# Half-height, 512-column weight loads and four-result projection blocks in a float32 decoder trunk with an interleaved expert layer

## The reference, cut to what matters

```python
def _layer(x, conv_buf, mem_k, mem_v, p):
    mo, new_buf, vn = _mixer(_rmsnorm(x, p['g_mix']), conv_buf, p)
    x = x + mo
    x = x + _cross_attn(_rmsnorm(x, p['g_xattn']), mem_k, mem_v, p['w_xq'], p['w_xo'])
    x = x + _peer(_rmsnorm(x, p['g_ffn']), p['w_pq'], p['sub_keys'], p['peer_u'], p['peer_v'])
    return x, new_buf, vn

def _mixer(h, conv_buf, p):
    proj = jnp.einsum('bld,dn->bln', h, p['w_in'])          # 1024 -> 7 * 1024
    b_g, c_g, h_a, u, v, g_a, g_b = jnp.split(proj, SPLITS, axis=-1)
    z = c_g * h_a                                           # short convolution over tokens, 3 taps
    ...
    o_a = jnp.einsum('blc,cd->bld', b_g * conv, p['w_a_out'])
    u = jax.nn.gelu(u)
    vn = _layernorm(jax.nn.gelu(v), p['sg_ln_g'], p['sg_ln_b'])
    s = _spatial_gate(vn, p['sg_w'], p['sg_b'])
    o_b = jnp.einsum('blc,cd->bld', u * s, p['w_b_out'])
    m = jax.nn.sigmoid(g_a) * o_a + jax.nn.sigmoid(g_b) * o_b
    return jnp.einsum('bld,de->ble', m, p['w_mix_o']), new_buf, vn
```

## Time and profile before

| | |
|---|---|
| median of 3 runs | 4949.3 us (4941.9 to 4970.75) |
| span of the profiled execution | 4944.5 us |
| PE busy | 3105.5 us (63%) |
| PEld busy | 2272.9 us (46%) |
| DVE busy | 3498.1 us (71%) |
| ACT busy | 452.5 us (9%) |
| POOL busy | 2890.5 us (58%) |
| moved by DMA | 1526.96 MB, mean 309 GB/s |

### The profile page before, as it was taken

How to read it: one execution, slowest core, us unless ns; L and a number is a source line. 1 busy time by engine, 2 the same in 40 slices (tenths; PEclk the granted TensorE clock), 3 DMA queues, 4 the chain that set the end, 5 groups by cost and what they waited for, 6 DMA issues and landing times. The chain is left out here.

```text
span 4944.5 us, 35593 instructions
## 1 busy us (share of the span) xinstructions
PE 3105.5 (63%) x11812; PEld 2272.9 (46%) x11812; DVE 3498.1 (71%) x6425; ACT 452.5 (9%) x956; POOL 2890.5 (58%) x2317
## 2 busy tenths in 40 slices
PE   8998469797878666667565458977897663000000
PEld 7887336575865224556455226655785221000000
DVE  2101678676657897875678897867647888888887
ACT  1001000021101001012010001011111000000000
POOL 0000156565646675765667765656546677877786
PEclk9999789898579887888777778988778886555555
DMA  5444479899979887999999987989979888999998
GB/s 190 142 152 136 135 274 334 319 382 349 329 269 377 312 301 260 394 374 362 337 352 369 366 298 251 381 323 395 351 248 330 304 320 296 344 343 353 356 347 298
DMA packets 604880, 1526.96 MB, mean 309 GB/s; under 512 B 43412, under 2 KB 293460, under 8 KB 604696
## 3 DMA queue, kind: packets, MB, share of 16 engines
q0 software_dynamic: 331776, 1208.11, 66.2%
q1 hardware_dynamic: 272920, 316.58, 18.9%
HBM read 1517.29 MB, written 7.23 MB: 308 GB/s over the span
## 5 line engine op out<-in xcount | busy, mean ns | idle before, releaser
L573 POOL DMA_INDIRECT urow<-in_peer_u_dram,idx x1152 | 1471.3, 1277 | 1469.0 <-DVE idx L1135 622.8
L573 POOL DMA_INDIRECT vrow<-in_peer_v_dram,idx x1152 | 1417.3, 1230 | 557.8 <-issue 343.2
L1025 DVE CUSTOM_DVE_ANT_0 urow<-urow,T 128x1024 f32<-128x1024 f32 x1152 | 1370.2, 1222 | 206.0 <-DMA urow<-in_peer_u_dram,idx 155.4
L612 PE MATMUL ps<-RH,W 128*128 128x256 f32 (+1 forms) x4608 | 1192.4, 420 | 268.4 <-DVE RB L1268 85.4
L1046 DVE SCALAR_TENSOR_TENSOR acc<-vrow,wts,acc 128x1024 f32<-128x1024 f32 x858 | 1101.9, 1284 | 136.1 <-DMA vrow<-in_peer_v_dram,idx 70.9
L612 PEld LDWEIGHTS ps<-RH,W 128*128 128x128 f32 x4608 | 904.4, 197 | 535.9 <-issue 109.2
L802 PE MATMUL ps<-vrow,RV 128*128 128x512 f32 x1152 | 628.3, 706 | 441.1 <-DVE RV L1036 402.2
L802 PEld LDWEIGHTS ps<-vrow,RV 128*128 128x128 f32 x1152 | 254.8, 228 | 812.3 <-issue 534.7
L826 ACT ACTIVATE gel<-dots 128x4 f32<-128x4 f32 x288 | 58.9, 204 | 2639.7 <-DVE dots L1025 2529.2
L625 PE MATMUL ps<-W,RB 128*128 128x256 f32 (+1 forms) x1152 | 264.0, 393 | 40.9 <-DVE RB L1298 23.9
L612 PE MATMUL ps<-RB,W 128*128 128x256 f32 (+1 forms) x1024 | 266.0, 414 | 17.0 <-DMA W<-in_w_b_out_dram 16.0
(11 more groups left out here) (175 smaller groups left out, 2234.3 us busy)
## 6 DMA issues: line engine op xcount, KB each, us to landing
W<-in_w_in_dram SPq DMA_DIRECT2D x112, 1024.0 KB
W<-in_w_pq_dram SPq DMA_DIRECT2D x32, 1024.0 KB
urow<-in_peer_u_dram,idx POOLq DMA_INDIRECT x1152
vrow<-in_peer_v_dram,idx POOLq DMA_INDIRECT x1152
W<-in_w_a_out_dram SPq DMA_DIRECT2D x16, 1024.0 KB
W<-in_w_b_out_dram SPq DMA_DIRECT2D x16, 1024.0 KB
W<-in_w_mix_o_dram SPq DMA_DIRECT2D x16, 1024.0 KB
W<-in_w_xq_dram SPq DMA_DIRECT2D x16, 1024.0 KB
```

Of the source, the lines that this page charges most:

```text
L573: pool.indirect_dma_start(ring[:, j, :], None, table, bass.IndirectOffsetOnAxis(ap=idx[:, q % TSLOT, e:e + 1], axis=0)).then_inc(landed[j] ...
L612: m = pe.matmul(pf(name), slot(u)[:, k, (c % 2) * P:(c % 2) * P + P], src[:, k, 0:ncols(name[0] % 2)], start=(k == 0), stop=(k == KC - 1))
L1025: dve.tensor_tensor_reduce(urow[r, j, :], urow[r, j, :], T[r, kept, :], 1.0, 0.0, ALU.mult, ALU.add, dots[r, j:j + 1]).then_inc(u_read, 1)
```

## The change

Each load holds 512 columns and half of the contraction's rows: `UW = 512`, `KH = 4` row blocks. It is still 1 MiB, each row in HBM is 2 KiB. `project` forms a block of four results (`BLK = 4`) of one kind: it waits for four banks, then runs the first unit (row blocks 0 to 3) for all four results and then the second (row blocks 4 to 7), so that the four results are finished one after another in the second half. In the plan the first job of a block costs 5/2 of a result's cost, each other one 1/2. The kinds alternate by blocks: c, h, b, u for results 0 to 3, and then for 4 to 7, and ga, oa, gb, ob in the same way. `project_tokens` uses 512 moving columns.

The buffers follow: c goes to F1 in place of two buffers `cs`, the convolution is worked in F1, ga goes to mT, gb to four buffers `cs`, the query results `qp` lie in RV with four buffers in place of two; ACT no longer waits for DVE between c and h, nor between ga and oa. The number of ACT and DVE instructions is not changed.

```diff
-UW = 256
+UW = 512
+KH = KC // 2
+BLK = 4
 SLOTS = 6
-UF = KC * UW
+UF = KH * UW
...
-    for c in range(KC):
-        jobs += [(("c", c), "act", 1, fm), (("h", c), "dve", 1, fm), (("b", c), "dve", 1, fm), (("u", c), "act", 1, fm)]
+    def block(kind, a, owner):
+        return [((kind, BLK * a + i), owner, 1, fm / 2 if i else 5 * fm / 2) for i in range(BLK)]
+
+    for a in range(2):
+        jobs += block("c", a, "act") + block("h", a, "dve") + block("b", a, "dve") + block("u", a, "act")
...
-    for h in range(PH):
-        if h + 1 < PH:
-            jobs += [(("pq", 2 * h + 2), "act", 1, fm), (("pq", 2 * h + 3), "act", 1, fm)]
-        jobs += [(("sc", h), "act", 2, 2)]
+    jobs += block("pq", 0, "act")
+    for a in range(PH // 2):
+        if 2 * a + 2 < PH:
+            jobs += block("pq", a + 1, "act")
+        jobs += [(("sc", 2 * a), "act", 2, 2), (("sc", 2 * a + 1), "act", 2, 2)]
...
+    def add_block(p, kind, a):
+        add(p, kind, 2 * a, kind, BLK * a)
+        add(p, kind, 2 * a + 1, kind, BLK * a + BLK - 1)
...
-                    c0 = part * DM + n * UW
-                    src = A[name][layer_of(p), :, c0:c0 + UW].rearrange("(k p) n -> p k n", p=P)
+                    c0, r0 = part * DM + n // 2 * UW, n % 2 * KH * P
+                    src = A[name][layer_of(p), r0:r0 + KH * P, c0:c0 + UW].rearrange("(k p) n -> p k n", p=P)
...
+            def project(p, kind, a, src):
+
+                block = [(p, kind, BLK * a + i) for i in range(BLK)]
+                for name in block:
+                    begin(name)
+                for r in range(2):
+                    u = (p, kind, 2 * a + r)
                     await_unit(u)
-                for k in range(KC):
-                    m = pe.matmul(pf(name), slot(u)[:, k, (c % 2) * P:(c % 2) * P + P], src[:, k, 0:ncols(name[0] % 2)],
-                                  start=(k == 0), stop=(k == KC - 1))
-                end(m)
+                    for i, name in enumerate(block):
+                        for k in range(KH):
+                            m = pe.matmul(pf(name), slot(u)[:, k, i * P:(i + 1) * P],
+                                          src[:, KH * r + k, 0:ncols(p % 2)],
+                                          start=(r == 0 and k == 0), stop=(r == 1 and k == KH - 1))
+                        if r:
+                            end(m)
...
-                        for k in range(KC):
-                            m = pe.matmul(ps[0:rows, BANK[name] + a, b * UW:(b + 1) * UW],
-                                          src[:, k, i * P:i * P + rows], slot(u)[:, k, :],
-                                          start=(k == 0), stop=(k == KC - 1))
+                        for k in range(KH):
+                            m = pe.matmul(ps[0:rows, BANK[name] + a, :],
+                                          src[:, KH * r + k, i * P:i * P + rows], slot(u)[:, k, :],
+                                          start=(r == 0 and k == 0), stop=(r == 1 and k == KH - 1))
...
-                for c in range(KC):
-                    if c >= 2:
-                        emptied((p, "h", c - 2))
-                    evac((p, "c", c), cs[c % 2][:, 0:n], pf((p, "c", c)))
-                    evac((p, "u", c), F2[:, c, 0:n], pf((p, "u", c)), ACT.Gelu_apprx_tanh)
+                for a in range(2):
+                    for c in range(BLK * a, BLK * a + BLK):
+                        evac((p, "c", c), F1[:, c, 0:n], pf((p, "c", c)))
+                    for c in range(BLK * a, BLK * a + BLK):
+                        evac((p, "u", c), F2[:, c, 0:n], pf((p, "u", c)), ACT.Gelu_apprx_tanh)
```

More of the change, by code:

```diff
@@ L96, in phase_jobs @@
     jobs += [(("n", 1, i), "dve", 2, 2 if i else 14) for i in range(nt)]
-    jobs += [(("q", c), "act", 1, fm) for c in range(KC)]
+    jobs += block("q", 0, "act") + block("q", 1, "act")
     jobs += [(("s", 0), "act", 2, 4), (("s", 1), "act", 2, 4), (("pt", 0), "act", 2, 6)]
@@ L172, in plan_units @@
             add(p, "v", n, "v", nt - 1)
-        for n in range(4):
+        for a in range(2):
             for kind in "chbu":
-                add(p, kind, n, kind, 2 * n + 1)
-        for n in range(4):
+                add_block(p, kind, a)
+        for a in range(2):
             for kind in ("ga", "oa", "gb", "ob"):
-                add(p, kind, n, kind, 2 * n + 1)
+                add_block(p, kind, a)
         for n in range(4):
@@ L184, in plan_units @@
                     add(p, kind, n, kind, MC - 1)
-        for n in range(4):
-            add(p, "q", n, "q", 2 * n + 1)
+        for a in range(2):
+            add_block(p, "q", a)
         if g:
@@ L193, in plan_units @@
             add(p, "xo", n, "xo", nt - 1)
-        for h in range(PH):
-            add(p, "pq", h, "pq", 2 * h + 1)
+        for a in range(PH // 2):
+            add_block(p, "pq", a)
     return units, last
@@ L305, in decoder_step @@
         tmp = TMP[:, 340:340 + NM]
[L306 removed]
+        cs = [TMP[:, i:i + NM] for i in (0, 660, 980, 1300)]
         sgw = TMP[:, 0:DM].rearrange("p (g s) -> p g s", g=KC)
@@ L654, in trunk @@
                     project_tokens((p, "v", i), hT, i, rows)
-                for c in range(KC):
+                for a in range(2):
                     for kind in "chbu":
-                        project((p, kind, c), c, hT)
+                        project(p, kind, a, hT)
                 if g:
@@ L671, in trunk @@
                 await_evac(pe, (p, "mx", KC - 1))
[L672 to L676, removed]
+                for a in range(2):
+                    project(p, "ga", a, hT)
+                    project(p, "oa", a, F1)
+                    project(p, "gb", a, hT)
+                    project(p, "ob", a, F2)
                 await_evac(pe, (p, "ob", KC - 1))
@@ L694, in trunk @@
                 norm_transposes(1)
-                for c in range(KC):
-                    project((p, "q", c), c, hT)
+                for a in range(2):
+                    project(p, "q", a, hT)
                 await_evac(pe, (p, "q", KC - 1))
@@ L777, in trunk @@
                 norm_transposes(2)
-                for c in range(2):
-                    project((p, "pq", c), c, hT)
+                project(p, "pq", 0, hT)
                 for h in range(PH):
-                    if h + 1 < PH:
-                        for c in (2 * h + 2, 2 * h + 3):
-                            project((p, "pq", c), c, hT)
+                    if h % 2 == 0 and h + 2 < PH:
+                        project(p, "pq", h // 2 + 1, hT)
                     begin((p, "sc", h))
@@ L896, in trunk @@
                     act.wait_ge(zlo_out, 32 * (l + 1))
[L897 to L902, removed]
+                    act.wait_ge(vn_out, 16 * (l + 1))
+                emptied((p, "b", KC - 1))
+                for a in range(2):
+                    for c in range(BLK * a, BLK * a + BLK):
+                        evac((p, "ga", c), mT[:, c, 0:n], pf((p, "ga", c)), ACT.Sigmoid)
+                    for c in range(BLK * a, BLK * a + BLK):
+                        if a:
+                            emptied((p, "ob", c - BLK))
+                        evac((p, "gb", c), cs[c % BLK][:, 0:n], pf((p, "gb", c)), ACT.Sigmoid)
                 if not g:
@@ L957, in trunk @@
                 for h in range(PH):
-                    for c in range(0 if h == 0 else 2 * h + 2, min(2 * h + 4, 2 * PH)):
-                        evac((p, "pq", c), qp[c // 2 % 2][:, c % 2, 0:n], pf((p, "pq", c)))
+                    if h % 2 == 0:
+                        for c in range(0 if h == 0 else 2 * h + 4, min(2 * h + 8, 2 * PH)):
+                            evac((p, "pq", c), qp[c // 2 % 4][:, c % 2, 0:n], pf((p, "pq", c)))
                     name = (p, "sc", h)
@@ L1216, in trunk, with short_conv @@
                 ts = tmp[:, GC:NM].rearrange("p (b n) -> p b n", b=NSEQ)
-                for c in range(KC):
+                def short_conv(c):
                     def tap(j):
@@ L1251, in trunk @@
                         dve.wait_ge(zl_done, KC * l + c + 1)
-                    take((p, "b", c))
-                    done(dve.tensor_tensor(F1[:, c, 0:n], pf((p, "b", c)), tmp[:, 0:n], ALU.mult))
-                    emptied((p, "b", c))
+                for a in range(2):
+                    for c in range(BLK * a, BLK * a + BLK):
+                        short_conv(c)
+                    for c in range(BLK * a, BLK * a + BLK):
+                        take((p, "b", c))
+                        done(dve.tensor_tensor(F1[:, c, 0:n], pf((p, "b", c)), F1[:, c, 0:n], ALU.mult))
+                emptied((p, "b", KC - 1))
                 dve.wait_ge(sgb_in, 16 * (p + 1))
```

62 lines of the change are left out of this document (29 added, 33 removed).

## The result

The changed kernel takes 4992.6 us as a median (4975.7 to 5011.3, 6 runs) against 4952.9 (4937.6 to 4970.8, 6 runs) for the kernel before on the same chip: a ratio of 1.0072, 95% interval 1.004 to 1.0105. It is slower, by about 36 us, where I had forecast 4895 and a range up to 4950. Run again later it gave 1.0065 (1.0039 to 1.009). The profiled execution of the changed kernel has a span of 4974.0 us and a time of 4975.7 us.

A forecast was written before the change was run, and what follows sets the result against it. PE was taken to bound trunk 0, DMA trunk 2, with trunks 1 and 3 losing time to late loads. Trunk 0 -1, trunks 1 and 3 -16 each, trunk 2 -21: together -54 us, median 4895 us, range 4845 to 4950.

The forecast's parts named there:

- The moved group: Before mo: plan rounding puts one more group between DVE's last ob results, losing 9, 11, 9 us in trunks 1, 2, 3.
- The signs that I had named for being wrong: Trunks: the forecast is wrong if PE waits for DVE at h or ob by blocks, or trunk 2 doesn't shrink.
- Turns of 2 KiB and the store, -24 a trunk: c to mx, trunks 1 and 3: faster loads end 13.4 us of DVE waits; the earlier state's store saves 11.
- Can DVE alone be that quick?: c to mx, trunk 1: 11 groups at 10.5 us plus 37 us of own work let DVE finish by 937 to 942.
- the waits only change names: Trunks 1 to 3: DMA bounds all, faster loads slow the gathers, only 12 us saved, 4937 us; chance 0.17.
- The queues take turns by row: DMA queues: bytes split by row size, 3.5 to 1 before; 2 KiB rows make it 2 to 1, q1 131 GB/s.
- Cheaper rows, -7: Trunk 2, c to ob: 2 KiB rows save 7.4 ns per pair of rows, 7.5 us; bounds 0 and 15.
- my line: DMA row price: straight line through both queues' packet costs, 47.3 ns for 1 KiB and 87.2 for 2 KiB.
- The memory rows, -25: Trunk 2, mo's start: fewer, faster loads ahead of ACT's memory rows take 25 us off DVE's 27.7 us gelu wait.
- Later first results, 0: Block starts: DVE and ACT wait up to 6.4 us more for a block's first result; costed at nothing.
- my slow rival of 5010 us: Block handovers in trunks: DVE waits 6.4 us more at 18 places, 115 us in full, giving 5010 us; chance 0.12.
- 512 columns: PE matmuls: one of 512 columns replacing two of 256 saves 8.8 ns, 1.4 us in trunk 0, 1.3 in 1 and 3.

The follow-up runs named there:

- x_ob7_back: Changed kernel with no expert group between the last two ob results in trunks 1 to 3: 4955.9 us, ratio 0.9996 to the kernel before.
- x_moved: Kernel before with one more expert group ahead of the last ob result in trunks 1 to 3: 4967.5 us, ratio 1.0006.
- x_rows1k: Changed kernel with each load issued as two transfers of 256 columns, so rows of 1 KiB: 4977.9 us, ratio 1.0036 to the kernel before.
- x_plan_rows1k: Changed kernel with even job costs in the plan and rows of 1 KiB: 4966.5 us, ratio 1.0023 to the kernel before.
- x_tall: Changed kernel's block order and buffers, but full-height loads and matmuls of 256 columns, results one by one, even plan costs: 4949.8 us, ratio 0.9968 to before.
- x_tall_costs: Block order with full-height loads of 256 columns, but the changed kernel's plan costs of 5/2 and 1/2: 4962.1 us, ratio 1.0004 to before.
- x_mix: Block order, even costs, full-height 256-column projection loads; half-height loads and 512 moving columns for v, mo, k, vv, xo: 4932.6 us, ratio 0.9944 to before.
- x_plan: Changed kernel with every job of a block costing the same in the plan: 4956.0 us, ratio 0.998 to the kernel before.
- x_plan_ob7: Changed kernel with even plan costs and one group put between the last two ob results in trunks 1 to 3: 4985.4 us, ratio 1.0061 to before.
- x_light: Changed kernel with c, h, b, u loads of trunks 1 to 3 fetching only the first half of their rows: 4959.3 us, ratio 0.9991 to before.
- x_last: Changed kernel with a block's whole plan cost on its last job: 4985.0 us, ratio 1.0055 to the kernel before.
- x_tokens: Kernel before with half-height loads and 512 moving columns for v, mo, k, vv and xo only: 4943.6 us, ratio 0.9961.

## Why the prediction was wrong

The table holds, from the start times of PE's matmuls, the stages that differ, in us. "c to mx" runs from the first c matmul to the first ga matmul, "mo to xo" from first to first, "xo to selection" from xo's last matmul to the first of the selection. "Group taken back" is x_ob7_back. The second profile of each of the two kernels shows how far one profile can be trusted.

| | before | before again | changed | changed again | group taken back |
|---|---|---|---|---|---|
| c to mx, trunk 1 | 195.9 | 192.2 | 185.1 | 185.6 | 185.9 |
| c to mx, trunk 3 | 195.0 | 192.7 | 181.6 | 184.8 | 184.8 |
| c to mx, trunk 2 | 207.1 | 204.2 | 212.5 | 212.1 | 211.3 |
| gap, trunks 1, 2, 3 | 1.2, 3.4, 1.2 | 1.2, 3.4, 1.2 | 16.3, 22.6, 16.2 | 16.8, 23.2, 17.3 | 5.0, 11.8, 3.4 |
| mo to xo, trunk 2 | 262.8 | 254.6 | 242.4 | 245.9 | 250.1 |
| xo to selection, trunks 1 to 3 | 415.1 | 415.2 | 422.2 | 427.2 | 427.3 |
| after trunk 3 and its selection | 797.1 | 808.7 | 813.5 | 816.8 | 819.7 |

*The moved group* was found, and priced by the right mechanism for this kernel: 9 + 9 + 11 = 29 us, against 34 to 40 measured. The size was short because I took the three earlier ob results as emptied when they were ready. In the timeline above they wait for the group before them until 1099.96, are done 2.4 us after PE's end, and the group, with the addition of its sum to X, takes 12.9 us and not 10.5: 2.4 + 12.9 + 1.0 = 16.3. In trunk 2 the plan puts a group after the first of the four results as well, hence 22.6. The price isn't the group's alone: in the kernel before (x_moved) the same group cost -6 to +12 us. There its profile loses 8 us in each of trunks 1 and 3 and gains some 6 to 14 in trunk 2, as below.

*The step that failed* is the gains. I summed them to -83 us (two times -24 from loads and the store, -7 for rows, -25 for the memory rows, -3 for columns); x_ob7_back has all of them without the moved group, and its ratio is 0.9996 with an interval from -12 to +8 us. The signs that I had named for being wrong both came: PE waits for DVE at h (15.9 us in trunk 1), and trunk 2 didn't shrink. Against the means of the two profiles before, the stages of x_ob7_back up to its last selection, with its ga to ob of trunk 2 (147 for 152), add up to +2 us; the stages from mo to xo of trunks 1 and 3 are left out, for the reason in the last section.

For c to mx the profiles with the block order fall in two sets, by the rows that they load: five with 1 KiB, at half height (x_rows1k, x_plan_rows1k) or full height (x_tall, x_tall_costs, x_mix), and five with 2 KiB (changed, changed again, x_ob7_back, x_plan, x_plan_ob7). Left out are x_light, which loads less, and x_last, whose groups lie otherwise. In us:

| c to mx | before, two profiles | blocks, 1 KiB rows | blocks, 2 KiB rows |
|---|---|---|---|
| trunks 1 and 3 | 192 to 196 | 189 to 191 | 182 to 186 |
| PE's waits for loads there | 10 to 13 | 0 | 0 |
| ACT's wait for the state's store | 23 to 24 | 25 to 27 | 0 (once 12) |
| DVE's waits for gathered rows there | 2 to 3 | 11 to 13 | 17 to 22 |
| trunk 2 | 204 to 207 | 205 to 208 | 211 to 216 |
| DVE's waits for gathered rows in trunk 2 | 14 | 21 to 23 | 27 to 32 |

What the queues moved from c to mx of trunk 1 in the kernel before, 771.4 to 967.3 us (packets, MB, share of 16 engines):

```profile
q0 software_dynamic: 13318, 48.47, 65.2%
q1 hardware_dynamic: 20916, 21.31, 32.5%
```

Piece by piece:

- *Turns of 2 KiB and the store, -24 a trunk.* The waits went, as written, but c to mx gained by the means of the profiles only 9 us in trunk 1 and 10 in trunk 3. The block order took PE's waits for loads away by itself, and was worth 3 to 4 us; the longer rows took the store's wait away, and were worth 5 to 7 more. "Can DVE alone be that quick?" was the faulty line: I gave a group 10.5 us from a stretch in which nothing waited for gathers, and never asked for the bytes. The 69.8 MB above are 406 GB/s in the forecast's 172 us, more than the 388 that I had called all that DMA gives. At 388 they take 180 us, so by my own figure a third of the 24 was out of reach. The changed kernel moved them at 377, in 185 us.

  With loads no longer late, gathers are: 18.6 us from c to u in trunk 1. x_light showed that part of this wait follows the loads' traffic. This is in the main my rival "the waits only change names", though not through the turn of queues at 2 to 1 that I gave for it: q1 moved 5.01 MB in 60 us, no more than the 5.25 before. "The queues take turns by row" is not borne out: packets at 1.9 to 1 mean that q1 had no work for part of that stretch, or that the rule is another.
- *Cheaper rows, -7.* The price itself is right: q1 took 18.9% of 4944.5 us before and 17.5% of 4974.0 after, 64 us less of all engines' time for the same 316.58 MB, or 7%. In the 60 us stretches 85.8 ns against 2 x 46.6 is 8%, and 6% per byte, as the mean packets are 1980 and 1007 bytes. (By my line it was 7.8%, not the 7.6 that I wrote.) The Trainium skill (DMA: Bandwidth & Descriptors, section "Why small descriptors are slow") gives, as an estimate from its cycles, 4% for the longer row; the measurement decides. But the time is not returned: c to mx in trunk 2 grew by 5 to 8 us, its ga to ob shrank by 4 to 7, and the table above puts the growth with the rows: with 1 KiB rows it is not there. What in the longer rows makes the gathers late is open.
- *The memory rows, -25.* ACT's wait for them fell from 32.4 us to 15.9, and DVE's for the gelu behind it from 27.7 to 0.3. In x_ob7_back ACT's wait is 18.0 us and DVE's is this:

```profile
2333.92 0.16 DVE L1048 TENSOR_TENSOR wts<-gel,gate 128x4 f32<-128x4 f32 x1 [10.00 <-ACT gel L842]
```

  So DVE waits 17.7 us less, but the gap of trunk 2 is still 8.4 us longer than before, and gap and mo to xo together are 261.9 us against 266.2 and 258.0 in the two profiles of before: of the 25 us none is seen in the time. In the changed kernel the moved group fills the same hole that the quicker memory rows close, so the two can't be added; I had added them. x_moved shows it from the other side: the old kernel with only the group moved has 1.8 us in place of 27.7 there, and gap and mo to xo of trunk 2 together at 13.9 + 238.3 = 252.2 us, so in that trunk it gains.
- *Later first results, 0.* From xo to the selection the changed kernel takes 7 to 12 us more and x_tall 4 us less (126.3 + 158.3 + 126.5). That is the query projections, where results come late in their block; that too few groups cover them is argued. x_last, which takes the groups from between a block's results, is slower than x_ob7_back by 29 us, and takes 446 us from xo to the selection, 19 more than x_ob7_back. So the term is small but not nothing; my slow rival of 5010 us, with 18 places at 6.4 us, isn't what happened. From ga to ob in trunks 1 and 3 PE stayed the limit, at 140 us, as said.
- *512 columns*, 1 us a trunk, are beyond what the profiles can tell apart.

*The stretch after trunk 3* holds nothing of the change, and is 797 us in one profile of the kernel before and 809 in the other, in which each gather takes POOL some 25 ns more. Over all the kernels run here it lies between 795 (x_rows1k) and 820 (x_tall, x_ob7_back). The seven profiles of kernels with 2 KiB rows throughout lie from 809 to 820, with a mean of 814, the ten others from 795 to 820, with a mean of 807; nothing in the edits explains such a difference. So the 16 us that separate the first profiles of before and changed there can't be put down to the change as a whole; whether some of them belong to it stays open, since no kernel was profiled often enough.

The whole-run waits of DVE sum it up, before, then changed, then x_ob7_back:

```profile
DVE wts L1028 <- ACT gel L826: 280.6, 274, 27.7
DVE urow L1025 <- DMA urow<-in_peer_u_dram,idx: 155.4, 240, 5.8
DVE X L1287 <- PE ps L625: 122.3, 13, 26.6
...
DVE acc L1046 <- DMA vrow<-in_peer_v_dram,idx: 70.9, 148, 2.4
```

```profile
DVE urow L1043 <- DMA urow<-in_peer_u_dram,idx: 215.0, 275, 5.5
DVE wts L1046 <- ACT gel L840: 199.9, 285, 13.2
DVE X L1312 <- PE ps L641: 175.8, 19, 26.2
DVE acc L1064 <- DMA vrow<-in_peer_v_dram,idx: 122.1, 207, 1.9
```

```profile
DVE urow L1045 <- DMA urow<-in_peer_u_dram,idx: 232.8, 305, 3.2
DVE wts L1048 <- ACT gel L842: 222.4, 288, 13.6
DVE X L1314 <- PE ps L643: 129.7, 17, 26.3
DVE acc L1066 <- DMA vrow<-in_peer_v_dram,idx: 128.7, 212, 2.7
```

Before to changed, the gelu waits lose 81 us and the waits for gathers gain 111; the wait for mo's and xo's results gains 54, of which 46 go when the one group is taken back.

Why x_mix is the best of all is only argued: the block order with full-height loads (x_tall) gains 10 to 16 us, in part from c to mx (2 to 6 us less in trunk 1) and the queries, and the token kinds with half-height loads (x_tokens) another 19; together 28. Each part was timed alone, what in it earns the time was not, and the profile of x_tokens doesn't show where its 19 us lie: gap and mo to xo of its trunk 2 are 266 us together, no less than before.

## What to carry to other kernels

When a plan rounds planned cost to whole pieces of other work, work out by hand where each piece falls around the last results before a barrier: one group of 11 to 13 us there cost 34 to 40 us over three trunks, in a kernel whose four last results come in a burst, and nothing measurable in the kernel before. A wait that is removed gives back only what the next-late thing allows: before counting it, divide the bytes that the stage must move by the time that you forecast for it, and compare with the best rate that the trace shows. Two edits that fill the same hole in an engine's time are counted once.

## What the runs showed that I had not expected

The stretch from mo to xo of trunks 1 and 3 takes 274 to 280 or 284 to 289 us, whatever the kernel, and the difference lies in the sample scores, which have 128 matmuls of 8 columns each. Below are the instructions of every second sample, before and then changed, in trunk 1 (durations in ns, shortest, median, longest), and the row of their stretch in the columns of the earlier trace rows:

```profile
L725 PE MATMUL ps<-RB,KV x128: 175/361/361, 1246.6 to 1316.7; 128*128 128x8 f32 x128
...
1221.00:1342.00 121.00, 100.00 (x483) 95.21 (x481) 82.19 (x108) 25.60 (x56) 67.08 (x50) 0.62 0.87 316
```

```profile
L741 PE MATMUL ps<-RB,KV x128: 175/256/362, 1254.6 to 1309.6; 128*128 128x8 f32 x128
...
1229.00:1338.00 109.00, 85.54 (x482) 80.49 (x480) 82.30 (x109) 25.46 (x56) 68.06 (x52) 0.71 0.92 349
```

Just before, from 1200 to 1221 us, PE of the kernel before was busy without a pause at a granted clock of 1.00, that is 2.4 GHz; in these matmuls it falls to 1.2 GHz sooner or later, and that is worth 12 us a trunk. The changed kernel's second profile had them at a median of 361 ns too. Comparing two single profiles over such a stage says nothing on the change.
